# Order of value pages and weights on SyncE's queue in a hybrid decoder step

## What is computed

```python
past_k = cache_k[l][page_table]; past_v = cache_v[l][page_table]
s = einsum(q, k) * HEAD_DIM ** -0.5 + Fq - Fk        # forgetting attention
att = einsum(softmax(where(mask, s, NEG_INF)), v)
lru = gelu(gl) * rg_lru(causal_conv(xl))
x = x + concat(rms_norm(att), rms_norm(lru)) @ w_out
x = x + square(relu(rms_norm(x) @ w_up)) @ w_down
```

## Time and profile before

| What | Value |
|---|---|
| median of 3 runs | 2313.91 us (2313.5 to 2315.0) |
| the profiled execution, its own time | 2315.23 us |
| its span in the trace | 2313.6 us |
| PE / PEld busy | 98% / 95% |
| DVE / ACT / POOL busy | 69% / 37% / 7% |
| moved by DMA | 368.47 MB, mean 159 GB/s |
| DMA between some 230 us and 640 us | 310 to 330 GB/s |
| value page, SP's queue | 128 of 512 KB, median 6.5 us to landing |
| key page, POOL's queue | 128 of 512 KB, median 6.0 us to landing |
| `w_in` half unit, SP's queue | 82 of 512 KB, median 6.8 us to landing |

### The profile page before, as it was taken

How to read it: one execution, slowest core, us unless ns; L and a number is a source line. 1 busy time by engine, 2 the same in 40 slices (tenths; PEclk the granted TensorE clock), 3 DMA queues, 4 the chain that set the end, 5 groups by cost and what they waited for, 6 DMA issues and landing times.

```text
span 2313.6 us, 50019 instructions
## 1 busy us (share of the span) xinstructions
PE 2257.7 (98%) x19886; PEld 2198.2 (95%) x19886; DVE 1607.0 (69%) x2041; ACT 857.6 (37%) x1200; POOL 156.4 (7%) x195
## 2 busy tenths in 40 slices
PE   7999999999999999999999999999999999999996
PEld 6999898988988999999999999999999999999996
DVE  7359889988884597776676576576576566566563
ACT  5134443344344333243343243243243243243245
POOL 0001111111114031000000000000000000000002
PEclk9999999999999999999999999999999999999998
DMA  7358999999975342333433433433433433433432
GB/s 242 101 165 263 327 327 330 316 310 323 325 261 196 95 131 68 101 105 106 125 103 100 129 97 100 134 93 99 136 96 94 136 103 89 134 109 85 132 92 92
DMA packets 386828, 368.47 MB, mean 159 GB/s; under 512 B 12243, under 2 KB 350580, under 8 KB 385572
## 3 DMA queue, kind: packets, MB, share of 16 engines
q1 hardware_dynamic: 359684, 295.38, 41.7%
q0 software_dynamic: 18608, 67.64, 8.2%
q10 hardware_dynamic: 8448, 4.20, 0.6%
HBM read 354.22 MB, written 12.94 MB: 159 GB/s over the span
## 4 chain that ended last, share of the span: by engine, by line
PE 84%; DVE 7%; issue 3%; DVEq 2%; ACT 1%; DMA 1%; SPq 1%; POOL 0%; ACTq 0%; POOLq 0%
PE PS L1889 36%; PE PS L1893 17%; PE PS L2335 9%; PE PS L2334 9%; PE PS L2333 9%; DVE KR L1344 2%; PE PS L2050 2%; DVE SC L1346 1%; DVEq L1499 1%; PE PS L2098 1%; DVE WL L1208 1%; PE PS L2240 1%; DVE NM L1498 0%; ACT WH L745 0%; DMA VR<-in_cache_v 0%
## 5 line engine op out<-in xcount | busy, mean ns | idle before, releaser
L1091 ACT ACTIVATE WH<-RAW 128x1024 fp32r<-128x1024 f32 x293 | 304.6, 1056 | 679.1 <-PE PS L1893 521.5
L1638 DVE TENSOR_TENSOR WL<-RAW,WH 128x1024 fp32r<-128x1024 f32 x293 | 358.2, 1223 | 133.8 <-ACT WH L1091 132.1
L1889 PE MATMUL PS<-XH,WH 128*128 128x260 f32 x1952 | 409.1, 291 | 21.4 <-DVE XL L1273 7.3
L1889 PE MATMUL PS<-HH,WH 128*128 128x260 f32 x2048 | 412.4, 282 | 1.3 <-issue 0.6
L1893 PE MATMUL PS<-HH,WL 128*128 128x260 f32 x2048 | 411.6, 282 | 0.0
L1889 PE MATMUL PS<-HL,WH 128*128 128x260 f32 x2048 | 410.8, 282 | 0.0
L1889 PE MATMUL PS<-XL,WH 128*128 128x260 f32 x1952 | 394.4, 284 | 0.0
L1893 PE MATMUL PS<-XH,WL 128*128 128x260 f32 x1952 | 394.0, 283 | 0.0
L1741 DVE TENSOR_TENSOR A<-A,PS 128x520 f32<-128x520 f32 x256 | 177.5, 695 | 264.6 <-PE PS L1893 263.7
L1889 PEld LDWEIGHTS PS<-XH,WH 128*128 128x128 f32 x1952 | 301.9, 190 | 39.9 <-issue 22.9
L1889 PEld LDWEIGHTS PS<-HH,WH 128*128 128x128 f32 x2048 | 314.6, 188 | 1.8 <-issue 1.1
(11 more groups left out here) (338 smaller groups left out, 3089.9 us busy)
## 6 DMA issues: line engine op xcount, KB each, us to landing
KR<-in_cache_k POOLq DMA_DIRECT2D x128, 512.0 KB, 6.0
VR<-in_cache_v SPq DMA_DIRECT2D x128, 512.0 KB, 6.5
RAW<-in_w_up SPq DMA_DIRECT2D x128, 512.0 KB, 4.2
RAW<-in_w_down SPq DMA_DIRECT2D x128, 512.0 KB, 4.5
RAW<-in_w_in SPq DMA_DIRECT2D x82, 512.0 KB, 6.8
RAW<-in_w_out SPq DMA_DIRECT2D x32, 512.0 KB, 6.0
TMP<-in_w_up SPq DMA_DIRECT2D x30, 512.0 KB, 6.0
xT_spill<-A SPq DMA_DIRECT2D x1, 4160.0 KB, 16.2
```

The costliest lines, as they stand in the source:

```text
L1091: nc.scalar.activation(RING_H[SLOT[i]], RB[b], ACT.Copy).then_inc(f_hi, 1)
L1638: V.tensor_tensor(RING_L[SLOT[i]], RB[op_block(i)], RING_H[SLOT[i]].bitcast(F32), ALU.subtract).then_inc(f_lo, 1)
L1889: mm(dsts[c], wh(k), x[:, k, c * HT:(c + 1) * HT], start=first and n == 0 and x is xh, stop=False)
```

## The change

In `step` of SP's program the two later value pages of each quarter move ahead of the unit's weights (and, in the second quarter, of the two gate loads). Nothing is added or taken away: the same DMAs, waits and sizes in another order.

```diff
                 for q in range(4):
                     if q == 0 and prev and older:
-                        values(i - 2, range(12, 14))
+                        values(i - 2, range(12, NPG))
                     if q and prev:
-                        values(i - 1, range(4 * q - 4, 4 * q - 2))
+                        values(i - 1, range(4 * q - 4, 4 * q))
                     if head:
                         src = [lambda: cols(w_in_v, COL_X + P * i), lambda: cols(w_in_v, COL_G + P * i),
@@
                         sp.dma_start(GW[:, 1, :], w_gate_x[0, one(i), :, :].rearrange("a p c -> p (a c)")).then_inc(gw_full, 16)
-                    if q == 0 and prev and older:
-                        values(i - 2, range(14, NPG))
-                    if q and prev:
-                        values(i - 1, range(4 * q - 2, 4 * q))
                 if not head:
                     load_unit(U_O + 6, 0, out_cols(6))
                     values(i - 1, range(12, NPG))
```

## The result

The changed kernel takes 2318.26 us (median of 20 runs, 2315.32 to 2322.37); the kernel before takes 2314.24 us (20 runs, 2313.19 to 2316.14). The ratio is 1.0017 with a 95% interval of [1.0011, 1.0023], so the change costs 4.0 us, between 2.5 and 5.3 us. The forecast was 2315.5 us, +1.6 us. The direction and the place were right and the size was less than half of what was measured.

A forecast was written before the change was run, and what follows sets the result against it. The prediction took PE, busy 98% of the span, as the bound. 0 for the steps and +1.6 us for the tail (+2.2 - 0.6), on the median of 2313.9 us, gave 2315.5 us; range 2311.4 to 2320.6 us.

The forecast's parts named there:

- The steps, cost 0: In the steps' four quarters, the later weights still arrive within the slack of their readers: 0 us.
- burst of 14.6 us: In the steps, two pages and two weight halves take 14.6 us from first issue to last landing.
- Late keys: Rival: third-quarter key pages meet pages and weights and delay DVE, 4.9 us over seven steps, 2320.4 us; chance 0.12.
- The tail's mechanism: Last call: O4 lands 7.3 us late, delaying ACT's queue and unit 3's tile; +2.2 - 0.6 = +1.6 us.
- estimate by the Trainium skill's page: In the tail, 6.8 us for the 2 MB burst, O4 landing at 727.6, no stop: -2.3 us; not adopted.
- PE stands 2.2 us: In the tail, PE waits at 740.0 for unit 3's tile, freed at 742.2: a 2.2 us stop.
- two late keys a step: In the steps, the late-key delay hitting two keys in each step: over 2330 us.
- slow burst with late keys: Upper end of the range: O4's slow landing in the tail plus the cheap form of late keys, 2320.6 us.
- pages win: Rival, tail: O4 lands by 728.3 and PE loses its page waits, -2.3 us, 2311.6 us; chance 0.14.
- Slow burst: Rival, tail: O4 needs the full 14.6 us, +5.8 us, 2319.7 us; chance 0.08.

The follow-up runs named there:

- e1: The new order in the steps only, the last call in the order of the kernel before: 2314.36 us, ratio 0.9999 to the kernel before.
- e2: The new order in the last call only, the steps in the order of the kernel before: 2317.57 us, ratio 1.0014.
- e5: The whole change, plus pages 12 to 15 ahead of O6 in the last call: 2318.15 us, ratio 1.0019 to the kernel before.
- e11: The changed kernel once more under another name, for a second trace: 2317.42 us, ratio 1.0013 to the kernel before.
- e10: The kernel before once more under another name, for a second trace: 2314.01 us, ratio 0.9996.
- e4: The kernel before with, in the last call, pages 10 and 11 ahead of O5 and 12 to 15 ahead of O6: 2312.11 us, ratio 0.9991.
- e6: The whole change, but in the last call O4 ahead of pages 6 and 7, and pages 12 to 15 ahead of O6: 2314.30 us, ratio 1.0002.
- e7: As e5, but ACT copies O4 after the squares and head copies instead of ahead of them: 2314.09 us, ratio 1.0001 to the kernel before.
- e8: As e4, but ACT frees the first tile of output unit 1 before the exponentials: 2311.59 us, ratio 0.9988 to the kernel before.
- e3: The whole change, but in the last call O4 goes ahead of pages 6 and 7, as before: 2318.37 us, ratio 1.0018 to the kernel before.
- e9: The whole change, but in the last call O4 behind pages 8 and 9 too, and pages 10 to 15 ahead of O6: 2321.55 us, ratio 1.0029.

## Why the prediction was right or wrong

**The steps, cost 0: right.** e1 shows it, and the 467.3 us from first to last gates. The burst of 14.6 us was too pessimistic: in the step followed it took at most 11.5 us (first page out at 402.5, second half out at 404.8 and landed 9.2 us later), and ACT's copy in the first quarter was not even late.

**Late keys: fell.** No DVE wait on a key page, and the slowest landed in 7.8 us.

**The tail's mechanism: right in each link.** O4's second half was to land 7.7 us after an issue at 722.8. In the trace it went out at 723.4 and took 8.1 us:

```profile
L440 SPq DMA_DIRECT2D RAW<-in_w_out x2: 434/470/507, 722.9 to 723.4; - x2
...
DMA to landing us min/median/max: 6.2/7.2/8.1
```

ACT's copy was to be 7.3 us late; it waited 7.61, 6.52, 7.27 and 6.61 us in the traces of the change, e2, e5 and e11. PE's stop was to be 2.2 us; it is 2.8 to 2.9, as PE, with no page wait ahead of it, arrives earlier at the same stop. Of the page waits, 2.3 us in the first trace of before, 0.7 stayed in that of the change and none in e2 and e11, where the prediction let about 0.7 stay. The predicted +1.6 us stands against +1.2 to +1.3 us by the traces' waits. The estimate by the Trainium skill's page, 6.8 us for the burst, would have had O4 in time. The trace decides against it: O4's second half by itself took 8.1 us, and the burst 10.1 us from page 6 (out at 721.4), between the page's 6.8 and the 14.6 of the steps.

**The size was off by a term that the sum lacked.** The step that fell short is "PE stands 2.2 us" taken as the price of the stop. A stop costs its length and, in three of the four traces that have it, a low stretch behind it. Four traces have the stop of 2.8 to 2.9 us at unit 3's tile with at most one page wait of 0.7 us ahead of it: in e2, e5 and e11 the granted clock behind it is 0.66 to 0.83 in a stretch or two of 5 us, 1.7 us of full-speed time each; in the changed kernel's first trace it is 1.00. None of the seven other traces in which PE stands under 2.5 us in all near 740 us (before, e10, e1, e4, e6, e7, e8) has a low stretch there. Three in four of 1.7 us is an estimate of 1.3 us, and 1.2 + 1.3 = 2.5 us lies at the lower end of the measured 2.5 to 5.3 us and amid the 0.9 to 5.3 of e11.

Four traces are few, but the clock is on record for every run. Its mean over the span is 0.9907 in the 20 runs of the change and 0.9903, 0.9909 and 0.9906 in e2, e5 and e11, against 0.9912 to 0.9914 in the runs of before beside the experiments. A difference of 0.0005 to 0.0009 of 2315 us is 1.2 to 2.1 us at full speed. It doesn't say where in the span the clock is lost, but it bears out the size. With the 1.2 us of waits that makes 2.4 to 3.3 us, against medians of +2.7 to +4.0 us in the four comparisons. What is left, some 1.5 us in the first pair, stays open. The start doesn't explain it: up to the first gates all 13 traces run the same program and take 197.5 to 200.7 us, and e11, 3.4 us above e10, has the third shortest start.

The row was there to be read. The trace of before has such a stop near 703 us, with its low stretch behind it, and the prediction puts nothing of it into the price:

```profile
703.76 0.48 PE L1889 MATMUL PS<-XH,WH 128*128 128x260 f32 x2 [2.81 <-ACT A L780]
```

```profile
705.00:710.00 5.00, 5.00 (x32) 5.00 (x31) 3.96 (x4) 2.03 (x4) 3.58 (x2) 0.66 0.00 0
```

Three of the prediction's figures don't follow from its own terms: two late keys a step make 9.8 us and 2325.3 us, not over 2330; a slow burst with late keys at 4.9 us makes 2324.6 us, not 2320.6; and "pages win" is 2311.6 us, not the 2311.4 of the range. None of them bears on the result.

**Two delays side by side: not seen.** The prediction counted O6 before page 12 and the tile stop in one sum, and rightly had the one hide most of the other. It did not say that O4 put right alone would change nothing; e3 shows that, by longer page waits and the lower clock behind them. The change has two faults in the last call, each of which is enough.

**The rivals.** "Pages win" had its gain of 2.3 us only in e4 (-2.4 us), another order of the queue, and there half of the page waits stayed; in e6, where they shrank to 0.3 us, the median shows no gain. "Slow burst" fell with the landing of 8.1 us.

## What to carry to other kernels

Ask of a moved load not only whether its reader has slack, but what stands behind the reader's wait in the in-order queue of its engine: here the copy of O4 could start at 732.55 instead of 723.19 without harm (e7), but a tile's release stood behind it. Before moving loads past others in a queue, go through each place where two waits meet there; putting one right may only lay bare the next (e3). And price a PE stop near 3 us with the clock behind it: look at the granted clock behind a stop of the same length that is already in the trace.

## What the runs showed of the hardware

A stop of equal length does not always have the same price. The best case is one that no experiment touches: in all 13 traces PE stands 2.8 us near 683 us for a VectorE product. In eight of them a low stretch follows, in five it doesn't. PE and the clock in the first trace of before, then in its second:

```profile
682.58 0.50 PE L1889 MATMUL PS<-XH,WH 128*128 128x260 f32 x2 [2.79 <-DVE XL L1236]
```

```profile
680.00:685.00 5.00, 2.35 (x17) 2.17 (x18) 4.03 (x8) 3.08 (x6) 0.00 (x0) 1.00 0.83 288
```

```profile
682.58 0.80 PE L1889 MATMUL PS<-XH,WH 128*128 128x260 f32 x2 [2.78 <-DVE XL L1236]
```

```profile
680.00:685.00 5.00, 2.42 (x11) 2.42 (x12) 4.03 (x8) 2.39 (x4) 0.00 (x0) 0.76 0.83 290
```

The stop near 704 us, which all kernels but e8 have, is 1.9 to 2.9 us long and has its low stretch in seven of twelve traces. All low stretches from 678 to 765 us, each of 1.7 us of full-speed time:

| trace | near 683 | near 706 | behind 740 | tail's length, us |
|---|---|---|---|---|
| before | | x | | 94.01 |
| e10 (before again) | x | | | 92.06 |
| e1 | | x | | 93.42 |
| change | | | | 93.83 |
| e11 (change again) | x | | x | 94.64 |
| e2 | x | | x | 94.89 |
| e5 | | x | x | 96.50 |
| e3 | x | x | x | 97.34 |
| e9 | x | | two | 101.01 |
| e4 | | x | | 92.62 |
| e6 | x | x | | 92.17 |
| e7 | x | x | | 92.69 |
| e8 | x | no stop | | 89.88 |

Two traces of one kernel can so differ by 2 us in the tail, half of what the change costs; one pair of traces doesn't decide on such a difference. The start differs in the same way: between 20 and 40 us the mean granted clock is 0.83 in the first trace of before and 0.66 in its second, with the same program (and yet both reach the gates at 198.5 us). The Trainium skill, in "TensorE: Matmul & The Clock Gate", Part 1, says that the gate follows how busy the array has been, and that its watch is not set to the kernel's start; the traces agree as far as the low clock follows stops and comes with the same stop in one execution and not in the next.

Two pages ahead in the queue hardly lengthen the landing of a weight half. In the tail, where no key pages run beside it, each of O4's halves of 512 KB took 5.9 to 8.1 us from issue to landing behind two pages (the change, e2, e5, e7, e11), against 6.0 and 7.7 us without them.
